# Turning the gated retention heads: TensorE transposes against 32x32 VectorE blocks and a DRAM scratch

## The reference

```python
ret = head_rmsnorm(retention(rq, rk, rv)).reshape(b, s, RET_WIDTH)   # RET_WIDTH = 4 heads * 128 = 512
ret = jax.nn.silu(rg) * ret
moba = moba_attention(...).reshape(b, s, MOBA_WIDTH)                 # 512 columns
mix = jnp.concatenate([ret, moba], axis=-1) @ w_out[layer]           # (256, 1024) @ (1024, 1024)
x = x + rmsnorm(mix, post_mix_norm[layer])
h = rmsnorm(x, pre_ffn_norm[layer])
f = (jax.nn.silu(h @ w_gate[layer]) * (h @ w_up[layer])) @ w_down[layer]
x = x + rmsnorm(f, post_ffn_norm[layer])
```

## Time and profile before

| | us |
|---|---|
| median of 3 runs | 304.81 (304.76 to 305.1) |
| the profiled execution | 305.12 |
| its span, first to last instruction | 303.3 |
| PE busy in it | 296.6 (98%), 1456 matmuls |
| DVE, ACT, POOL busy | 184.4, 155.0, 12.0 |
| DMA | 58.35 MB, mean 192 GB/s |

### The profile page before, as it was taken

One profiled execution on the slowest core, in us unless ns is written; L12 is line 12 of the kernel. 1 busy time (PEld: TensorE's weight loads), 2 busy tenths in 40 slices (PEclk: granted clock), 3 DMA queues, 4 the chain that ended last, 5 costly groups with the idle time before them and its releaser, 6 DMA issues.

```text
span 303.3 us, 4177 instructions
## 1 busy us (share of the span) xinstructions
PE 296.6 (98%) x1456; PEld 240.1 (79%) x1456; DVE 184.4 (61%) x274; ACT 155.0 (51%) x254; POOL 12.0 (4%) x20
## 2 busy tenths in 40 slices
PE   8999999999999999999999999999999999999992
PEld 3788877787888888887888888888888888888881
DVE  2967566796877879797356464546355464551146
ACT  4989476736482747495253353544352443630331
POOL 0030000000020013200000000000000000000001
PEclk9999999999999999999999999999999999999997
DMA  6999996218627441569846454654747454600003
GB/s 182 404 407 384 410 357 209 70 37 295 214 81 259 147 149 64 213 215 390 292 146 214 156 191 152 202 191 162 253 138 243 156 199 157 193 19 0 2 0 138
DMA packets 17545, 58.35 MB, mean 192 GB/s; under 512 B 2003, under 2 KB 2556, under 8 KB 17532
## 3 DMA queue, kind: packets, MB, share of 16 engines
q1 hardware_dynamic: 17136, 57.06, 53.4%
q0 software_dynamic: 304, 1.06, 1.0%
q10 hardware_dynamic: 92, 0.05, 0.1%
HBM read 57.10 MB, written 1.06 MB: 192 GB/s over the span
## 4 chain that ended last, share of the span: by engine, by line
PE 90%; DVE 7%; ACT 1%; issue 1%; DVEq 0%; POOL 0%; ACTq 0%
PE bank L977 26%; PE bank L979 26%; PE bank L978 26%; DVE w_lo L886 3%; PE bank L987 2%; PE bank L1025 2%; PE bank L1009 1%; PE bank L1029 1%; PE bank L1033 1%; PE bank L996 1%; PE bank L1092 1%; PE bank L1137 1%; DVE d_lo L893 1%; DVE res L968 1%; DVE res L962 1%
## 5 line engine op out<-in xcount | busy, mean ns | idle before, releaser
L977 PE MATMUL bank<-w_hi,a_hi 128*128 128x512 f32 x256 | 101.0, 394 | 0.0
L979 PE MATMUL bank<-w_hi,a_lo 128*128 128x512 f32 x256 | 99.9, 390 | 0.0
L978 PE MATMUL bank<-w_lo,a_hi 128*128 128x512 f32 x256 | 99.6, 389 | 0.0
L977 PEld LDWEIGHTS bank<-w_hi,a_hi 128*128 128x128 f32 x256 | 48.1, 188 | 10.4 <-issue 0.7
L979 PEld LDWEIGHTS bank<-w_hi,a_lo 128*128 128x128 f32 x256 | 48.0, 188 | 10.3
L978 PEld LDWEIGHTS bank<-w_lo,a_hi 128*128 128x128 f32 x256 | 48.1, 188 | 9.8
L886 DVE TENSOR_TENSOR w_lo<-raw,w_hi 128x1024 fp32r<-128x1024 f32 x40 | 48.1, 1244 | 7.9 <-ACT w_hi L608 7.9
L692 DVE TENSOR_TENSOR w_lo<-raw,w_hi 128x1024 fp32r<-128x1024 f32 x32 | 37.8, 1221 | 12.5 <-ACT w_hi L467 12.5
L623 ACT ACTIVATE sil<-bank,rstd 128x256 f32<-128x256 f32 x22 | 10.4, 474 | 62.2 <-PE bank L979 60.1
L608 ACT ACTIVATE w_hi<-raw 128x1024 fp32r<-128x1024 f32 x40 | 40.1, 1053 | 0.0
L901 DVE SCALAR_TENSOR_TENSOR hid<-bank,rstd,sil 128x256 f32<-128x256 f32 x22 | 10.6, 483 | 46.3 <-ACT sil L623 46.3
(11 more groups left out here) (108 smaller groups left out, 260.4 us busy)
## 6 DMA issues: line engine op xcount, KB each, us to landing
raw<-in_w_gu SPq DMA_DIRECT2D x44, 512.0 KB, 4.4
raw<-in_w_dn SPq DMA_DIRECT2D x22, 512.0 KB, 4.2
raw<-in_w_in SPq DMA_DIRECT2D x20, 512.0 KB, 8.2
raw<-in_w_out SPq DMA_DIRECT2D x8, 512.0 KB, 3.8
raw<-in_w_in SPq DMA_DIRECT2D x8, 256.0 KB, 5.8
xs<-in_x SPq DMA_DIRECT2D x2, 512.0 KB, 8.2
bias<-bias_row POOLq DMA_DIRECT2D x1, 1024.0 KB, 10.2
out<-res SPq DMA_DIRECT2D x4, 256.0 KB, 2.0
```

Source lines behind the costliest of these rows:

```text
L977: pe.matmul(acc, hi, wh, start=first, stop=False)
L978: pe.matmul(acc, hi, wl, start=False, stop=False)
L979: return pe.matmul(acc, lo, wh, start=False, stop=last)
```

## The change

Instead of PE, the two 128x512 halves are turned by DVE in 32x32 blocks (`dve.transpose`, two instructions), which puts every block's contents in turned order but leaves the block in its band of 32 partitions. To bring blocks into place, SP writes the 512 KB to a DRAM scratch `m_rows` and, when that has landed, reads it back with four DMAs, one for each band of 32 destination partitions, in runs of 1 KB, into the `gate` tile, which is free by then. ACT and DVE then make `m_hi` and `m_lo` from `gate` (SBUF) and no longer from PSUM. Both halves of the tokens wait for all four reads. Partition 32q+i of block b now holds feature 128q+32b+i, so the first 512 rows of `w_out` are reordered on the host to match; the bytes loaded are as many as before.

```diff
+B, Q = 32, 4
@@ views
+        def in_squares(m):
+            return m[:, :, :].rearrange("p t c -> p (t c)").rearrange("p (q t c) -> p q t c", q=Q, t=NT)
+        def turned_mix(t):
+            return in_squares(gate)[:, :, t, :].rearrange("p q (b i) -> p b q i", i=B)
+        def of_squares(m, t):
+            return m[:, 0:RH, t * P:(t + 1) * P].rearrange("p b (q i) -> p b q i", i=B)
@@ SP
             for s in range(GU):
                 load(base + s, (base + s) % RAW, w_gu[s])
+                if s == 1:
+                    sp.wait_ge(mix_sq_ready, NT)
+                    sp.dma_start(m_rows, in_squares(ret).rearrange("p q t c -> p q (t c)")).then_inc(mix_sq_stored, 16)
+                if s == 2:
+                    sp.wait_ge(mix_sq_stored, 16)
+                    row = NT * RH * B
+                    for q in range(Q):
+                        sp.dma_start(in_squares(gate)[q * B:(q + 1) * B].rearrange("p q t c -> p q (t c)"),
+                                     bass.AP(m_rows.tensor, q * row, [[Q * row, B], [B * Q * row, Q], [1, row]])
+                                     ).then_inc(mixT_loaded, 16)
@@ ACT
-            for t, b in ((0, 1), (1, 0)):
-                act.wait_ge(mix_turned, t + 1)
-                act.activation(m_hi[:, 0:4, t * P:(t + 1) * P],
-                               wk[:, b, :].rearrange("p (b i) -> p b i", i=P), ACT.Copy
-                               ).then_inc(mhi_ready, 1)
+            act.wait_ge(mixT_loaded, 16 * Q)
+            for t in range(NT):
+                act.activation(of_squares(m_hi, t), turned_mix(t), ACT.Copy).then_inc(mhi_ready, 1)
@@ DVE, behind the two mix products and ahead of lo_in of units 28 to 31
+            dve.wait_ge(mix_ready, NT)
+            for t in range(NT):
+                dve.transpose(in_squares(ret)[:, :, t, :], mix[:, t, 0:CW].rearrange("p (q c) -> p q c", q=Q)
+                              ).then_inc(mix_sq_ready, 1)
@@ DVE, behind them and the gp product
-            for t, b in ((0, 1), (1, 0)):
+            for t in range(NT):
                 dve.wait_ge(mhi_ready, t + 1)
-                dve.tensor_tensor(m_lo[:, 0:4, t * P:(t + 1) * P],
-                                  wk[:, b, :].rearrange("p (b i) -> p b i", i=P),
-                                  m_hi[:, 0:4, t * P:(t + 1) * P].bitcast(F32), ALU.subtract
+                dve.tensor_tensor(of_squares(m_lo, t), turned_mix(t), of_squares(m_hi, t).bitcast(F32), ALU.subtract
                                   ).then_inc(mlo_ready, 1)
@@ PE
-            for t, b in ((0, 1), (1, 0)):
+            for t in range(NT):
...
-                pe.wait_ge(mix_ready, t + 1)
-                turn(wk[:, b, :], mix[:, t, 0:CW], 4, mix_turned)
             pe.wait_ge(mlo_ready, 1)
             for c in range(2):
                 mixer(0, 1, c).then_inc(wm_done, 1)
```

More of the change, by code:

```diff
@@ L75, in hybrid_layer @@
 def hybrid_layer(nc, xt, x, g_post_mix, g_pre_ffn, g_post_ffn, rel_bias,
-                 w_in, w_out, w_gu, w_dn, ident_c, rope_c, decay_c, bucket_c, bias_row, out):
+                 w_in, w_out, w_gu, w_dn, ident_c, rope_c, decay_c, bucket_c, bias_row, m_rows, out):
     with ExitStack() as ctx:
@@ L236, in hybrid_layer @@
         mix_ready = sem("mix_ready")
-        mix_turned = sem("mix_turned")
+        mix_sq_ready = sem("mix_sq_ready")
+        mix_sq_stored = sem("mix_sq_stored")
+        mixT_loaded = sem("mixT_loaded")
         mhi_ready = sem("mhi_ready")
@@ L1308, in _laid_out @@
     up = a("w_up")[0].reshape(GU, KPU, P, NF, FG)
+    w_out = a("w_out")[0]
+    ret_rows = w_out[:RH * RV].reshape(Q, RH, B, D).transpose(1, 0, 2, 3).reshape(RH, P, D)
     return {
@@ L1317, in _laid_out @@
         "w_in": w_in.transpose(3, 0, 2, 1, 4).reshape(N_IN, P, UNIT),
-        "w_out": a("w_out")[0].reshape(NK, P, D)[WOUT_K],
+        "w_out": np.concatenate([ret_rows, w_out[RH * RV:].reshape(NK - RH, P, D)])[WOUT_K],
         "w_gu": np.stack([gate, up], 4).transpose(3, 0, 2, 1, 4, 5).reshape(NF * GU, P, UNIT),
@@ L1332 @@
     args["bias_row"] = nc.dram_tensor("bias_row", (MH, REV), F32, kind="Internal").ap()
+    args["m_rows"] = nc.dram_tensor("m_rows", (P, Q, NT * RH * B), F32, kind="Internal").ap()
     args["out"] = nc.dram_tensor("out", (S, D), F32, kind="ExternalOutput").ap()
```

## The result

The changed kernel takes 308.67 us, median of 9 runs (306.72 to 309.63), against 304.94 for the kernel before in the same rounds. The ratio is 1.0111, 95% interval 1.009 to 1.0133: slower by 1.1%, 3.7 us. The forecast was 305.5 with a range to 308.0, so the direction was right and the time lies outside the range. It is rival D, a long round trip with a clock that falls behind it, to which I had given 0.20 (0.10 with the clock). The profiled execution took 309.63, the slowest of the nine, so the steps read from it are at their long end.

A forecast was written before the change was run, and what follows sets the result against it. PE was taken to bound the kernel, its stream having no holes. Two removed turns (-0.89) plus a stall (+1.6) gave +0.7 us on the median 304.81: 305.5 us, range 304.2 to 308.0.

The forecast's parts named there:

- rival D: Store, reads or DVE transposes slow: PE 1.7 to 3.7 us late, 306.5 to 308.5, with clock to 311; chance 0.20.
- What bounds the kernel: PE, busy 98% of the span, a stream without holes; any hole put into it goes onto the end.
- The gain of the removed turns: Two turns of mix on PE, at 92.51 and 98.42, no longer issued: 0.89 us, the most the change can give.
- Step 1: DVE transposes behind the gated products, from 90.09: done at 91.4, bounds 91.2 and 92.6.
- Step 2: SP's store of half a megabyte to the scratch: 2.65 us, bounds 2.0 and 4.9, landed at 94.1.
- Step 4: ACT and DVE make m_hi and m_lo behind the reads' landing: 1.4 to 1.45 us, PE starting at 99.5.
- the moved steps: DVE splits of units 28 to 31 pushed back 1.3, SP loads some 3.7 us late; claimed to cost nothing.
- step 3: Four scratch reads, issued 0.47 apart: 3.9 us from first issue, landed at 98.05, ends 97.3 and 100.0.
- Rival A: The forecast's own case: PE stalls 1 to 2.5 us on two DMA landings in series, 304.9 to 306.4; chance 0.45.
- The stall: PE waiting for the turned retention heads, from 97.9 to 99.5: 1.6 us.
- The 0.443 between PE's first matmuls: Spacing of PE's first ten matmuls, taken as the lower clock level (1.2 GHz), in place of 0.227.
- the 0.6 us for the ports: Reads to 32 partitions reach 8 of 16 SBUF ports, landing some 0.6 us later; not included in the sum.

The follow-up runs named there:

- e5_nodma: Changed kernel without any of its DMAs, m_hi and m_lo made straight from what DVE turned, blocks not put in place: 304.10 us against 305.15 before.
- e6_dve: Kernel before with the two DVE transposes added behind the mix products, their output unused: 304.95 us, before 304.80.
- e4_nostore: Changed kernel without the store, the four reads taking the same pattern from a weight tensor in DRAM: 303.68 us, ratio to before 0.9961.
- e12_warm_hold: Changed kernel with loads of units 35 to 37 held until the reads landed, and 8 extra matmuls before PE's wait: 306.30 us, ratio to before 1.0052.
- e2_hold: Changed kernel with the loads of units 35, 36 and 37 issued only when the four reads have landed: 308.10 us, ratio to before 1.0096.
- e13_again: Changed kernel once more, unedited, for a second trace: 308.71 us, ratio to before 1.0122.
- e10_plain_hold: Changed kernel with one 128-partition read in 4 KB rows, blocks not placed, loads of units 35 to 37 held: 307.90 us, ratio to before 1.0078.
- e1_warm: Changed kernel with 12 extra bf16 matmuls on PE in front of its wait for the first m_lo: 307.26 us, ratio to before 1.0066.
- e3_wide: Changed kernel with one 512 KB read to all 128 partitions in 1 KB runs, blocks not put in place: 308.19 us, ratio to before 1.0108.

## Why the prediction was wrong

Right, step by step, with the number forecast and the one measured in the profile of the changed kernel:

- What bounds the kernel, and that a hole in PE's stream goes onto the end: the account above closes to 0.1 us.
- The gain of the removed turns: 0.9, measured 1.05 in `e5_nodma` with 0.9 in its interval.
- Step 1, the DVE transposes: done at 91.4, measured 91.54 (two for 1.32), with the start 0.1 late.
- Step 2, the store: 2.65, measured 2.79, and 2.7 to 2.8 in the other runs.
- Step 4, m_hi, m_lo and PE's start: 1.45 behind the landing, measured 1.43 (100.28 to 101.71).
- Nothing on the moved steps cost anything: the pushed-back splits in `e6_dve` and `e5_nodma`, the late loads in the changed kernel itself, where PE has no second new wait. The load of unit 35 landed 5.7 us after its issue and not 4.4.

Wrong: step 3, the reads, forecast 3.9 from the first issue and measured 5.9 in the profiled execution, 5.9 and 5.4 in two other traces of the same DMAs. The term was built as "four issues are one load of the same bytes". It has two parts that were left out. The last of four issues starts 1.33 us behind the first (94.36 to 95.69), and a read of 128 KB then takes about as long as a quick load of 512 KB: 3.2 in `e4_nostore` and `e12_warm_hold`, 3.5 in `e2_hold`. That makes 4.5 to 4.8, 0.6 to 0.9 over the forecast. I had let the spacing of the issues be swallowed by the 3.9, which nothing in the rows supported; the upper end that I wrote down, the last issue plus 4.4, was the sound way to build the sum. The other part is about 1.1 us (5.4 to 5.9 against 4.5 to 4.8) that goes when the loads of units 35 to 37 are held. The prediction had looked at them only as the ones that would be late, not as traffic beside the reads they stand behind, though it had said that they are issued from 96.1 on, in the middle of the reads. Why such loads cost this here and nothing in `e4_nostore` stays open. Rival A called both landings "well known from rows"; for the reads no row was, as step 3 itself says.

The second error hangs on the first. The stall came to 3.7 and not 1.6, longer than the 2.4 us that PE had done nothing in the earlier trace rows before its clock fell, and the clock was lost in 7 of 9 runs, by their times. The forecast itself had no term for it. Its price under rival D was 2.5; it was 1.7 in the profile, 1.4 in the medians, and 2.8 in `e13_again`, where it stayed low longest. With both, the sum would have been 304.8 + 2.8 + 1.5 = 309.1. The stall by itself, with the clock kept, is 306.7 to 306.9, which the range held. The chance of 0.20 for D was too low: it treated a landing in the upper half of the rows as an exception, when there were two landings in series and one late engine of sixteen made a landing late in the changed kernel and in `e10_plain_hold`.

Two smaller slips in the working changed neither the sum nor a chance. The 0.443 between PE's first matmuls divides 4.43 us by ten, but ten starts have nine gaps and the 4.43 includes the length of the last; the gap is 0.42 to 0.43, as behind the wait in the changed kernel. That PE was at its lower level there was read off this spacing, for the granted clock of that stretch is given as 1.00. And the 0.6 us for the ports is stated without the step that leads to it from the 2.4 beside it.

## What to carry to other kernels

Where PE's stream has no holes, price a path through DRAM as a sum of landings, each at the upper half of what its rows show. Add the spacing of the issues to the last one's landing, and look at what is issued ahead of it and behind it. Compare the sum with the cover, here 7.8 us from the mix products to PE's need, before comparing it with the 0.9 us of PE work it saves. A stall of about 3 us cost 1.4 to 2.8 us more here where the clock fell behind it, and a few idle matmuls in front of the wait (12 in `e1_warm`, 8 in `e12_warm_hold`) kept the clock up in the traces of both.

## What the runs showed that was not expected

- The length of PE's wait does not decide alone whether the clock falls. It fell after waits of 2.1 (`e10_plain_hold`), 2.5 (`e2_hold`), 2.9 (`e13_again`) and 3.5 us; it stayed up in the profiled execution of `e3_wide` after one of 3.2. With waits of about that length the changed kernel kept its clock in 2 of 9 runs.
- 32-partition transfers of 32 KB from SBUF to SBUF landed 1.8 to 2.1 us after their issue. Reads of 128 KB from DRAM took 2.7 to 3.5, all but the last of the four in the traces with the scratch and loads behind (4.1 to 4.6).
- An issue on SP does not always take the same time: the reads of the scratch went out 0.47 us apart, the moves from SBUF to SBUF 0.64 with SP alone and 0.7 with ACT issuing beside it.
- POOL's copies of 32x256 took 1.33 us each (four in 5.32), ACT's 0.44 (four in 1.74), and DVE's four splits beside POOL's took 5.19 in place of 4.59.
